# A two-block fp32 transformer on one core: the first mixer opened on raw x, the second mixer's norm summed bank by bank, attention operands made earlier, one bank moved

## The reference, cut to what matters

```python
def rms_norm(x, g):
    return x * lax.rsqrt(jnp.mean(x * x, axis=-1, keepdims=True) + 1e-6) * g

# first block
proj = rms_norm(x, norm_mix_g) @ w_in
qa, ka, va, fa, cq, ckv, kr, ga, gb = jnp.split(proj, splits, axis=-1)
log_f = jax.nn.log_sigmoid(fa + b_forget)
ya = forgetting_attention(qa, ka, va, log_f)      # causal softmax of q.k/8 + sums of log_f, 8 heads of 64
qb = rms_norm(cq, q_a_norm_g) @ w_q_up            # latent attention: kv from ckv, rope on q and kr
yb = latent_attention(...)                        # 8 heads
merged = sigmoid(ga + b1) * (ya @ w_branch_a) + sigmoid(gb + b2) * (yb @ w_branch_b)
x = x + merged @ w_out
x = x + swiglu(rms_norm(x, norm_ffn_g))           # f0, hidden width 2816
x = rms_norm(x, norm_final_g)                     # the joint between the blocks
# second block
x = x + 0.5 * swiglu(rms_norm(x, ffn1_norm))      # f1
proj = rms_norm(x, mix_norm) @ w_in_2             # compressed, selected, window attention and retention
nsa_gates = jax.nn.sigmoid(g_a)                   # 48 gates per token
x = x + mixed(gates, attention, retention) @ w_out_2
x = x + 0.5 * swiglu(rms_norm(x, ffn2_norm))      # f2
return rms_norm(x, final_norm)
```

## Time and profile before

| | |
|---|---|
| median of 3 runs | 2279.26 us |
| profiled execution | 2276.63 us |
| its span | 2274.4 us |
| PE busy | 2169.6 us (95%) |
| DVE busy | 1184.3 us (52%) |
| ACT busy | 901.4 us (40%) |
| POOL busy | 456.4 us (20%) |
| HBM read, written | 202.31 MB, 18.87 MB |

### The profile page before, as it was taken

One profiled execution on the slowest core, in us unless ns is written; L12 is line 12 of the kernel. 1 busy time (PEld: TensorE's weight loads), 2 busy tenths in 40 slices (PEclk: granted clock), 3 DMA queues, 4 the chain that ended last, 5 costly groups with the idle time before them and its releaser, 6 DMA issues.

```text
span 2274.4 us, 28585 instructions
## 1 busy us (share of the span) xinstructions
PE 2169.6 (95%) x9980; PEld 1780.0 (78%) x9980; DVE 1184.3 (52%) x1966; ACT 901.4 (40%) x1540; POOL 456.4 (20%) x379
## 2 busy tenths in 40 slices
PE   6999999999999999999988999999998999999997
PEld 4877877788887888887867888888876778888786
DVE  4547673454443254443246778778767235444324
ACT  3344664333222142223123466676645334222222
POOL 2002244031110032220013701111144222111000
PEclk9998999999999999999998999999989999999999
DMA  3311225333333322333323412222254332332331
GB/s 134 93 46 52 84 72 183 102 93 101 95 99 102 101 84 93 95 99 102 100 79 119 141 56 75 79 70 75 90 194 135 119 111 93 93 97 96 107 97 65
DMA packets 68536, 222.89 MB, mean 98 GB/s; under 512 B 7808, under 2 KB 8064, under 8 KB 68064
## 3 DMA queue, kind: packets, MB, share of 16 engines
q1 hardware_dynamic: 50832, 182.08, 26.0%
q10 hardware_dynamic: 13728, 27.27, 3.4%
q0 software_dynamic: 3888, 12.39, 1.8%
HBM read 202.31 MB, written 18.87 MB: 97 GB/s over the span
## 4 chain that ended last, share of the span: by engine, by line
PE 80%; DVE 8%; ACT 4%; POOL 3%; issue 3%; DMA 1%; ACTq 0%; DVEq 0%; SPq 0%; POOLq 0%
PE bank L178 23%; PE bank L180 23%; PE bank L179 23%; PE bank L185 2%; PE bank L184 2%; POOL hid L543 2%; PE bank L1748 2%; DVE w_lo L152 2%; ACT w_hi L147 1%; DVE gn_r L2317 1%; DMA w_raw<-stream 1%; DVE xn_lo L466 1%; PE bank L240 1%; PE bank L677 1%; DVE xg L251 1%
## 5 line engine op out<-in xcount | busy, mean ns | idle before, releaser
L152 DVE TENSOR_TENSOR w_lo<-w_raw,w_hi 128x1024 fp32r<-128x1024 f32 x337 | 465.4, 1384 | 598.9 <-ACT w_hi L147 598.5
L178 PE MATMUL bank<-xn_hi,w_hi 128*128 128x512 f32 x1656 | 663.9, 401 | 34.6 <-POOL xn_lo L258 23.4
L180 PE MATMUL bank<-xn_hi,w_lo 128*128 128x512 f32 x1656 | 651.5, 393 | 0.0
L179 PE MATMUL bank<-xn_lo,w_hi 128*128 128x512 f32 x1656 | 651.1, 393 | 0.0
L147 ACT ACTIVATE w_hi<-w_raw 128x1024 fp32r<-128x1024 f32 x337 | 353.2, 1051 | 386.6 <-PE bank L180 251.7
L178 PEld LDWEIGHTS bank<-xn_hi,w_hi 128*128 128x128 f32 x1656 | 315.5, 191 | 107.5 <-issue 20.7
L180 PEld LDWEIGHTS bank<-xn_hi,w_lo 128*128 128x128 f32 x1656 | 314.3, 190 | 67.3
L179 PEld LDWEIGHTS bank<-xn_lo,w_hi 128*128 128x128 f32 x1656 | 315.2, 190 | 61.9 <-issue 0.7
L178 PE MATMUL bank<-h_hi,w_hi 128*128 (+1 forms) x528 | 205.9, 390 | 4.1 <-DVE hid L487 3.7
L179 PE MATMUL bank<-h_lo,w_hi 128*128 (+1 forms) x528 | 205.5, 389 | 0.0
L180 PE MATMUL bank<-h_hi,w_lo 128*128 (+1 forms) x528 | 205.4, 389 | 0.0
(11 more groups left out here) (387 smaller groups left out, 3100.7 us busy)
## 6 DMA issues: line engine op xcount, KB each, us to landing
w_raw<-stream SPq DMA_DIRECT2D x337, 512.0 KB, 3.6
spill_g<-gate_out ACTq DMA_DIRECT2D x16, 256.0 KB, 4.3
m_temps<-spill_g POOLq DMA_DIRECT2D x16, 256.0 KB, 3.2
x<-xt SPq DMA_DIRECT2D x2, 1024.0 KB, 6.0
x<-xt ACTq DMA_DIRECT2D x8, 256.0 KB, 4.3
spill_x<-x ACTq DMA_DIRECT2D x1, 2048.0 KB, 7.4
spill_ga<-ga_out ACTq DMA_DIRECT2D x8, 256.0 KB, 2.0
spill_rv_hi<-rv_hi_out ACTq DMA_DIRECT2D x8, 256.0 KB, 2.4
```

Of the source, the lines that this page charges most:

```text
L152: nc.vector.tensor_tensor(w_lo[:, slot, :], w_raw[:, slot % 2, :], w_hi[:, slot, :], ALU.subtract).then_inc(split_lo, 1)
L178: nc.tensor.matmul(to, a_hi, b_hi, start=start, stop=False, skip_group_check=True)
L179: nc.tensor.matmul(to, a_hi, b_lo, start=False, stop=False, skip_group_check=True)
L180: return nc.tensor.matmul(to, a_lo, b_hi, start=False, stop=stop, skip_group_check=True)
```

## The change

1. The first mixer has no norm ahead of it. ACT makes `xn_hi` from `x * gain` as the pieces of x arrive, DVE `xn_lo`; the first two chunks run by `pair_by_parts`. The squares are added on POOL and summed over the partitions by one matmul of ones in the middle of chunk 3, `norm_r` is made after that, and it is multiplied in where banks are taken out: in `qk_raw`, `c`, the forget rows, v (through `r_token`, four small transposes of `norm_r`) and both attentions' `gate_out`. q and k chunks use seven banks in turn instead of four. SP loads x in four pieces, between the first two weight chunks.
2. f1's last two chunks are summed output by output, as f2's are; `norm_r` for the second mixer is made there. The joint's scaling of x stands ahead of the last two `w_lo` on DVE.
3. The second mixer's operands come through four buffers (`squares`) instead of two, and its first two chunks run by `pair_by_parts`.
4. In the first attention the operands of the next two heads are made near the head of an even unit instead of at its end.
5. The gates' chunk of the second mixer goes to bank 3 and no longer waits for `ck_done`; PE waits for the gates' sigmoid behind the first of the next pairs of chunks.
6. `pair_by_parts` waits for the second chunk only where it uses it.

The diff, cut. `norm()` goes; of the new function the common lines are shown too.

```diff
+        def scaled_parts(gain):
+            m, b = norm_sems, count_up(scaled=KT, hi=KT, lo=KT)
             def act_part(act):
+                for k in range(KT):
+                    act.wait_ge(m["scaled"], b["scaled"] + k + 1)
+                    nc.scalar.activation(xn_hi[:, k, :], squares[:, k % 4, :], ACT.Copy).then_inc(m["hi"], 1)
             def dve_part(dve):
+                for k in range(KT):
+                    if k >= 4:
+                        dve.wait_ge(m["lo"], b["lo"] + k - 3)
+                    nc.vector.scalar_tensor_tensor(squares[:, k % 4, :], x[:, k, :], col[:, gain + k:gain + k + 1],
+                                                   norm_r[:], ALU.mult, ALU.mult).then_inc(m["scaled"], 1)
             def pool_part(pool):
+                for k in range(KT):
+                    pool.wait_ge(m["hi"], b["hi"] + k + 1)
+                    nc.gpsimd.tensor_tensor(xn_lo[:, k, :], squares[:, k % 4, :], xn_hi[:, k, :],
+                                            ALU.subtract).then_inc(m["lo"], 1)
+            return act_part, dve_part, pool_part, (m["hi"], b["hi"]), (m["lo"], b["lo"])
...
-                if not closing:
+                if not lb:
...
                 stream_down(act, high_part)
-                if closing:
+                last_of_stream(act, high_part)
+                if lb:
...
+                last_of_stream(dve, low_part)
...
-                if closing:
+                if lb:
...
                     highs(h, (0, 1))
-                    if latent and h + 2 < HEADS1:
+                    if h + 2 < HEADS1 and (latent or h % 2 == 0):
                         stage(act, h + 2)
...
-                    if not latent and h % 2 == 0 and h + 2 < HEADS1:
-                        stage(act, h + 2)
...
-                    nc.vector.tensor_copy(gate_out[:, h % 2, :], banks[3][:]).then_inc(s["cleared"], 1)
+                    nc.vector.tensor_tensor(gate_out[:, h % 2, :], banks[3][:], norm_r[:], ALU.mult).then_inc(s["cleared"], 1)
...
-                for j in range(8):
+                pair_by_parts(pe, fq, (banks[0], banks[1]), xn_hi, xn_lo, (m["hi"], nb["hi"]), (m["low"], nb["low"]))
+                for j in range(2, 8):
                     slot = ready(pe, fq, j)
-                    at_least(pe, a["qk"], j - 3)
-                    tile_chunk(slot, banks[j % 4][:], xn_hi, xn_lo, normed=(norm_done, list(range(KT))) if j == 0 else None
-                               ).then_inc(used, 1)
+                    if j == 7:
+                        pe.wait_ge(a["qk"], 1)
+                    for k in range(KT):
+                        if j == 3 and k == KT // 2:
+                            pe.wait_ge(m["added"], nb["added"] + KT - 1)
+                            nc.tensor.matmul(banks[7][:], ones[:], total_sq, start=True, stop=True,
+                                             skip_group_check=True).then_inc(m["summed"], 1)
+                        w = slice(k * P, (k + 1) * P)
+                        last = mm3(banks[j % 7][:], w_hi[:, slot, w], w_lo[:, slot, w], xn_hi[:, k, :], xn_lo[:, k, :],
+                                   k == 0, k == KT - 1)
+                    last.then_inc(used, 1)
+                pe.wait_ge(consts_in, 80)
+                pe.wait_ge(consts_made, 2)
                 for j in range(3):
                     slot = ready(pe, fc, j)
-                    pe.wait_ge(a["qk"], 4 + j + 2)
+                    pe.wait_ge(a["qk"], j + 2)
                     tile_chunk(slot, banks[1 + j][:], xn_hi, xn_lo).then_inc(used, 1)
+                pe.wait_ge(m["recip"], nb["recip"] + 1)
+                for tb in range(TB):
+                    last = nc.tensor.transpose(banks[7][:, tb:tb + 1], norm_r[0:1, tb * P:(tb + 1) * P], ident[0:1, 0:1])
+                last.then_inc(a["token"], 1)
...
+                for k in range(KT):
+                    if k in (0, 4):
+                        high_part(act, *place(0, k // 4))
+                    if k % 2 == 0:
+                        act.wait_ge(x_in[k // 2], 16)
+                    nc.scalar.activation(xn_hi[:, k, :], x[:, k, :], ACT.Identity,
+                                         scale=col[:, COLS["mix1"] + k:COLS["mix1"] + k + 1]).then_inc(m["hi"], 1)
+                ahead(high_part, act, fq, 0)
+                for k in range(KT):
+                    if k == 4:
+                        ahead(high_part, act, fq, 1)
+                    if k >= 4:
+                        act.wait_ge(m["added"], nb["added"] + max(k - 4, 1))
+                    nc.scalar.activation(squares[:, k % 4, :], x[:, k, :], ACT.Square).then_inc(m["squared"], 1)
+                ahead(high_part, act, fq, 2)
+                ahead(high_part, act, fq, 3)
+                act.wait_ge(m["summed"], nb["summed"] + 1)
+                nc.scalar.activation(norm_r[:], banks[7][:], ACT.Sqrt, bias=col[:, COLS["eps"]:COLS["eps"] + 1],
+                                     scale=1.0 / D).then_inc(m["root"], 1)
+                joint_root(act)
+                act.wait_ge(consts_in, 80)
...
+                for k in range(KT):
+                    if k in (0, 4):
+                        low_part(dve, *place(0, k // 4))
+                    dve.wait_ge(m["hi"], nb["hi"] + k + 1)
+                    gain = COLS["mix1"] + k
+                    nc.vector.scalar_tensor_tensor(xn_lo[:, k, :], x[:, k, :], col[:, gain:gain + 1], xn_hi[:, k, :],
+                                                   ALU.mult, ALU.subtract).then_inc(m["low"], 1)
+                joint_gains(dve)
+                for j in range(4):
+                    ahead(low_part, dve, fq, j)
+                dve.wait_ge(m["root"], nb["root"] + 1)
+                nc.vector.reciprocal(norm_r[:], norm_r[:]).then_inc(m["recip"], 1)
+                dve.wait_ge(m["recip"], nb["recip"] + 1)
+                dve.wait_ge(consts_in, 80)
                 for j in range(8):
-                    ahead(low_part, dve, fq, j)
+                    if j >= 4:
+                        ahead(low_part, dve, fq, j)
                     finished(dve, fq, j)
-                    nc.vector.tensor_copy(qk_raw[:, j, :], banks[j % 4][:]).then_inc(a["qk"], 1)
+                    nc.vector.tensor_tensor(qk_raw[:, j, :], banks[j % 7][:], norm_r[:], ALU.mult).then_inc(a["qk"], 1)
...
-                    nc.vector.tensor_copy(y1[:, 4 + j, :], banks[1 + j][:]).then_inc(a["c"], 1)
+                    nc.vector.tensor_tensor(y1[:, 4 + j, :], banks[1 + j][:], norm_r[:], ALU.mult).then_inc(a["c"], 1)
...
+                dve.wait_ge(a["token"], 1)
+                nc.vector.tensor_copy(r_token, banks[7][:, 0:TB]).then_inc(a["token"], 1)
...
-                    nc.vector.tensor_copy(v_raw[:, tb, :], banks[4 + tb][:]).then_inc(a["v"], 1)
+                    nc.vector.tensor_scalar(v_raw[:, tb, :], banks[4 + tb][:], r_token[:, tb:tb + 1], None, ALU.mult
+                                            ).then_inc(a["v"], 1)
...
-                pool.wait_ge(*norm_done)
+                for k in range(1, KT):
+                    pool.wait_ge(m["squared"], nb["squared"] + k + 1)
+                    if k > 1:
+                        pool.wait_ge(m["added"], nb["added"] + k - 1)
+                    nc.gpsimd.tensor_tensor(total_sq, squares[:, 0, :] if k == 1 else total_sq, squares[:, k % 4, :],
+                                            ALU.add).then_inc(m["added"], 1)
+                pool.wait_ge(m["added"], nb["added"] + KT - 1)
+                pool.wait_ge(consts_in, 80)
+                nc.gpsimd.tensor_copy(cumul[:], cumul_raw[:]).then_inc(consts_made, 1)
+                pool.wait_ge(m["low"], nb["low"] + KT)
...
-            parts.append((skip, skip, skip, tables_in))
-            parts.append(n_mix2)
+            parts.append((n_act, skip, n_dve, tables_in))
+            parts.append((skip, skip, skip, n_pool))
...
-                for kv in range(2):
-                    slot = ready(pe, fc, kv)
-                    tile_chunk(slot, banks[kv][:], xn_hi, xn_lo, normed=(norm_done, list(range(KT))) if kv == 0 else None
-                               ).then_inc(used, 1)
+                pair_by_parts(pe, fc, (banks[0], banks[1]), xn_hi, xn_lo, n_hi, n_lo)
...
-                pe.wait_ge(*ck_done)
-                tile_chunk(slot, banks[0][:], xn_hi, xn_lo).then_inc(used, 1)
+                tile_chunk(slot, banks[3][:], xn_hi, xn_lo).then_inc(used, 1)
...
-                pe.wait_ge(t["gate"], 1)
+                pe.wait_ge(*ck_done)
                 for c in range(8):
                     kv, part = c // 4, c % 4
                     kq_chunk(c)
                     if c == 0:
+                        pe.wait_ge(t["gate"], 1)
...
-            slots = [ready(pe, first, j) for j in range(2)]
+            slots = []
             for j in range(2):
+                slots.append(ready(pe, first, j))
...
-            sp.dma_start(col[:], cols[:, P:2 * P]).then_inc(x_in[0], 16)
-            for half in range(2):
```

(10 more changed lines are left out.)

123 lines of the change are left out of this document (33 added, 90 removed).

## The result

The changed kernel takes 2227.55 us (median of 4 runs, 2224.65 to 2230.04) against 2278.56 for the one before (4 runs): a ratio of 0.9779, 95% interval 0.9764 to 0.9795. Forecast were 2232, a range of 2222 to 2244, and faster. The profiled execution took 2224.65, its span is 2222.8 in place of 2274.4, so 51.6 us have gone where my sum had 46.8.

A forecast was written before the change was run, and what follows sets the result against it. PE, with 80% of the chain of waits, was taken as the bound. Terms 21.8 + 14.6 + 7.0 + 3.4 = 46.8 us gave 2229.8 by the profiled time, 2232.5 against the median; forecast 2232, range 2222 to 2244.

The forecast's parts named there:

- The head: Program start through chunk 3: with the norm off the path, a gain of 21.8 us, bounds 17 and 24.
- The first attention: Waits for `ks_lo` go (5.3) and clock returns (10.3), less one new stall (1): 14.6 us, bounds 4 and 17.
- 12.0 - 1.7 = 10.3 come back if the waits go: First attention, 150 to 250 us: of 12.0 us lost at half clock, all but one stretch's 1.7 return.
- rival A: First attention's clock doesn't come back, only 5.3 - 1 gained there: 2242 us, chance 0.17.
- 120 to 220 runs above 0.95: Sign in the first attention: PE's granted clock above 0.95 there; below 0.90 would be rival A.
- The second mixer's opening: Reciprocal 6.2 us earlier, chunk 1 ends at 1206.4 before 1212.2: 5.8 us; with the gates 7.0, bounds 3 and 14.
- By parts, PE then has about 32 products open: Second mixer's opening, after the last `xn_lo`: about 32 products left for PE, 7.3 us at full clock.
- The gates: Second mixer: the sigmoid wait of 4.7 us and 1.5 of clock go, but weights set the pace; 1.2 of 6.2 kept.
- ACT's waits for weights: Sign behind the gates: these waits (32.3 us in 14 loads) shrink in number, PE waiting for `w_lo` instead.
- The second merge: PE starts after the first `w_lo` instead of the second: 3.4 us, bounds 1.5 and 5.

The follow-up runs named there:

- The table load's experiment: The changed kernel with one 128 x 1 copy on ACT ahead of its first wait, so that ACT's table load is done earlier: one run, 2225.23 us.
- the one with the early squares: The changed kernel with the early table load and ACT's first four squares ahead of `w_hi` of chunk 2: 2227.90 us, ratio 0.9771.
- their experiment: The changed kernel with the gates' chunk in bank 0 again, behind `ck_done`, PE waiting for the sigmoid before the next chunk: 2229.31 us, ratio 0.9785.
- the first profile: The first of three profiled executions of the changed kernel, no further edit: 2224.65 us.
- the three sets of runs: The changed kernel timed three times without edit, against the kernel before: 2227.55, 2228.21 and 2230.51 us.
- the merges' step: The changed kernel with ACT making `w_hi` ahead of its wait for POOL's sum in both merges: 2214.24 us, ratio 0.9725.
- the faster `xn_lo`: The changed kernel with the second mixer's `xn_lo` subtracted on DVE, POOL idle meanwhile: one run, 2225.15 us.

## Why the prediction was right

The time came out within 5 us of the forecast. The mechanism was right for every wait that the change removes; what was mis-sized is the clock in the first attention and the number of products left open in the second mixer's opening, and the two errors have opposite signs. By its own steps:

- **The head.** Chunk 0 landed at 5.26 (4.7 forecast), but then came what I had left out: ACT's table load of 1.28 us, which I had taken as done and which here begins only when chunk 0 has landed. PE started at 9.04 in place of 7.2. It cost little: the products of chunk 1 were then ready to run without a pause, and both chunks were done at 21.4 (20.4). The first add of squares came at 18.3 (18), and the sum cost PE 0.9 us and less (1.6). Chunk 5 by my sum at 44.8, measured 45.3 to 45.6. The table load's experiment shows that an earlier start of PE is lost again within sixteen products, the one with the early squares that the adds cost some 1 us.
- **The first attention** is the step that was mis-sized: "12.0 - 1.7 = 10.3 come back if the waits go". The waits went whole (5.3). Of the clock's 11.7 us, 5.1 to 8.6 are still lost, at full PE occupation, in stretches that follow no wait. 9.3 us were gained in place of 14.2, midway between the forecast and the 4.3 of rival A. The sign that 120 to 220 runs above 0.95 failed in all but one of six windows (0.93, and 0.97 once), and none is below 0.90, rival A's sign. Why the clock falls there stays open.
- **The second mixer's opening** was mis-sized to the other side. The reciprocal came 6.4 us earlier (6.2) and the last `xn_lo` at 1163.4 + 34.3 = 1197.7 (1198.7). There two errors nearly cancel: a tile took 1.7 us and not 1.9, and POOL's first subtraction began 1.5 us behind the first scaling and not 0.6. The step that failed is "By parts, PE then has about 32 products open": the last `xn_hi` was ready 3.9 us before the last `xn_lo`, and PE had made hi products of chunk 1 meanwhile; 5.2 us or 23 products were left and not 7.7 us. Hence 9.0 and not 5.8.
- **The gates** gave 0.7 by the landmarks (-0.8, 1.4 and 1.4) and 1.8 by their experiment, 1.2 forecast, and the place where it is given back (a wait for `w_lo` one pair later) is the one named. ACT's waits for weights there did not shrink in number, as I had said they would: 32.7 us in 15 loads over the 88 us behind v's start, 32.3 in 14 before. **The second merge** gave 3.7, 3.4 forecast.
- **What no term had**: 2.6 us in places that weren't touched (0.4 and 1.9 in the table, 0.3 behind its last row), most of it clock in the first profile. The medians scatter likewise: 51.0, 48.7 and 44.0 us of gain in the three sets of runs, around a sum of 46.8.

## What to carry to other kernels

A norm at the head of a product can leave the path if its factor is one number per row of the output: multiply it in when the bank is taken out, where the copy costs the same 0.69 us anyway. An instruction on an in-order engine that waits for a slow neighbour should not stand ahead of one that feeds the bound; that one rule made the attention's part, the merges' step and, in the head, the squares. Price a removed wait by its own length first. What the clock gives back behind it differs by place: about half of the loss in the first attention, nearly all of it in the merges (12, 9 and 12 us down to 2). Read it from several executions. And look for a gain where the next bound stands: PE's earlier start at the head and the faster `xn_lo` were mostly lost again.

## What the hardware showed that I had not expected

TensorE fell to the lower of its two levels (1.2 in place of 2.4 GHz) in the first attention without a pause of its own: PE was busy for 50.0 of 50 us and had a mean granted clock of 0.93, and the stretches lay elsewhere in each of three executions, 5 to 9 us lost in all. In none of the three does a wait of PE over 0.1 us stand between 50 and 200 us. In the second mixer's opening PE ran at 0.67 over 18.7 us where it was given two products every 1.68 us, and at 0.91 over 18.0 us, in one execution, where it was given three a tile with longer pauses between. The kernel before had 0.62 with three a tile. What decides there is not shown.

In the program's first microseconds PE's products come 0.43 us apart (9.61 to 11.74) and then 0.23, while the column PEclk says 1.00 for both; the column misses that start.

ACT's first table load came only after the wait for chunk 0, 5.26 to 6.54, and the next instruction followed at 6.55. It need not stand there: in the kernel before it ran from 0.74 to 2.02, ahead of ACT's wait of 4.20 us for x, and with one small copy put first it ran at 0.74 in the changed kernel too. What places it behind the wait was not tried.
